# RWKV front on one Trainium2 core: the sigmoids of gates and decays in three rounds of two banks, up to four steps earlier, apart from lane 0's exponentials

## What is computed

```python
for d in range(2):                       # two directions
    w_log = -softplus(-(w0[d] + tanh(xw @ w1[d]) @ w2[d])) - 0.5
    decay = exp(-exp(w_log))             # = exp(-exp(-0.5) * sigmoid(...))
    a = sigmoid(a0[d] + (xa @ a1[d]) @ a2[d])
    k_d = k * (1.0 + (a - 1.0) * k_a)
kk = heads(k * k_k); kk = kk * rsqrt(max(sum(kk * kk), 1e-24))
# scan over 256 context and 512 own tokens, in each direction:
#   sa = S @ -kk_t
#   S = S * decay_t + outer(sa, kk_t * a_t) + outer(v_t, k_t)
#   y = S @ r_t
```

## Time and profile before

| what | value |
|---|---|
| time, median of 3 runs | 3779.27 us (3776.16 to 3779.83) |
| the profiled execution | 3782.2 us |
| its span | 3780.9 us |
| PE, DVE, ACT, POOL busy | 93%, 44%, 29%, 37% |
| granted TensorE clock, mean | 0.974 of full |
| the eight rounds of the RWKV scan | from about 2600 to 3292 us |
| a round, from one product L3413 to the next (2882.27, 2968.43, 3053.64) | 86.2 and 85.2 us |

### The profile page before, as it was taken

One profiled execution on the slowest core, in us unless ns is written; L12 is line 12 of the kernel. 1 busy time (PEld: TensorE's weight loads), 2 busy tenths in 40 slices (PEclk: granted clock), 3 DMA queues, 4 the chain that ended last, 5 costly groups with the idle time before them and its releaser, 6 DMA issues.

```text
span 3780.9 us, 72300 instructions
## 1 busy us (share of the span) xinstructions
PE 3527.5 (93%) x31740; PEld 2276.1 (60%) x31740; DVE 1656.9 (44%) x2942; ACT 1101.6 (29%) x2087; POOL 1389.0 (37%) x1239
## 2 busy tenths in 40 slices
PE   7998899999999989898999998999889888889998
PEld 3755674344554555554555554456667677658887
DVE  1246561465531234444242426524566665333334
ACT  3153331322205633423000002114555455220002
POOL 1230640233312245665324333344344444144443
PEclk9999899999999999999999999999999999999999
DMA  5341005311112135311111111331000000122222
GB/s 191 131 141 34 2 14 190 128 48 48 45 56 73 34 125 178 122 34 45 56 56 62 61 50 50 106 113 51 16 17 17 17 17 4 61 67 88 90 90 67
DMA packets 196434, 263.77 MB, mean 70 GB/s; under 512 B 6135, under 2 KB 151671, under 8 KB 194072
## 3 DMA queue, kind: packets, MB, share of 16 engines
q1 hardware_dynamic: 188960, 241.74, 19.2%
q10 hardware_dynamic: 7160, 17.41, 1.2%
HBM read 246.55 MB, written 12.58 MB: 69 GB/s over the span
## 4 chain that ended last, share of the span: by engine, by line
PE 55%; ACT 6%; DVE 4%; issue 2%; POOL 1%; DMA 0%; ACTq 0%; DVEq 0%; POOLq 0%
PE ps L241 44%; PE ps L3274 2%; PE ps L794 2%; ACT mem L871 1%; PE ps L385 1%; PE ps L821 1%; PE ps L809 1%; PE ps L492 1%; DVE mem L852 1%; ACT mem L3209 1%; PE ps L3833 1%; PE ps L3816 1%; ACT mem L881 0%; PE ps L501 0%; PE ps L3824 0%
## 5 line engine op out<-in xcount | busy, mean ns | idle before, releaser
L241 PE MATMUL ps<-mem 64*64 64x64 f32 (+4 forms) x25120 | 2620.6, 296 | 101.0 <-ACT mem L3209 28.3
L241 PEld LDWEIGHTS ps<-mem 64*64 64x64 f32 (+1 forms) x25120 | 1704.1, 151 | 1024.6 <-issue 522.9
L3139 POOL TENSOR_TENSOR mem<-mem 128x256 f32<-128x256 f32 (+1 forms) x264 | 230.6, 887 | 323.0 <-ACT mem L3709 167.3
L889 POOL TENSOR_SCALAR mem<-mem 128x768 f32<-128x768 f32 (+2 forms) x128 | 219.0, 1724 | 199.8 <-DVE mem L855 199.7
L2384 POOL TENSOR_TENSOR mem<-mem 128x512 f32<-128x512 f32 (+1 forms) x80 | 100.7, 1259 | 443.2 <-PE ps L241 367.2
L2397 ACT ACTIVATE mem<-ps 128x384 f32<-128x384 f32 (+1 forms) x80 | 35.6, 446 | 777.9 <-PE ps L241 735.6
L599 POOL TENSOR_TENSOR mem<-mem 128x512 f32<-128x512 f32 (+1 forms) x72 | 75.2, 1060 | 419.5 <-ACT mem L594 416.4
L2408 DVE TENSOR_TENSOR mem<-mem,ps 128x384 f32<-128x384 f32 (+1 forms) x80 | 39.9, 499 | 414.5 <-PE ps L241 414.5
L3274 PE MATMUL ps<-mem 128*128 128x128 f32 x960 | 168.3, 292 | 14.7 <-DVE mem L3198 11.0
L3198 DVE TENSOR_TENSOR mem<-mem,ps 128x256 f32<-128x256 f32 (+1 forms) x220 | 110.4, 514 | 127.7 <-PE ps L241 126.9
L3207 ACT ACTIVATE mem<-ps 128x256 f32<-128x256 f32 (+1 forms) x220 | 101.3, 460 | 188.0 <-PE ps L3274 187.7
(11 more groups left out here) (322 smaller groups left out, 3976.8 us busy)
## 6 DMA issues: line engine op xcount, KB each, us to landing
mem<-i_mod_w SPq DMA_DIRECT2D x48, 1024.0 KB, 6.9
mem<-i_ffn_wg SPq DMA_DIRECT2D x22, 1024.0 KB, 5.3
mem<-i_ffn_wu SPq DMA_DIRECT2D x22, 1024.0 KB, 5.4
mem<-i_e_w_in SPq DMA_DIRECT2D x16, 1024.0 KB, 6.1
mem<-i_o_w_in SPq DMA_DIRECT2D x16, 1024.0 KB, 5.4
mem<-i_ffn_wd SPq DMA_DIRECT2D x16, 1024.0 KB, 5.0
mem<-i_e_mod_w SPq DMA_DIRECT2D x12, 1024.0 KB, 12.3
mem<-i_o_mod_w SPq DMA_DIRECT2D x12, 1024.0 KB, 7.2
```

The source lines that it names most:

```text
L241: ins = e.h.matmul(out, l, r, start=(i == 0), stop=(i == n - 1))
L889: K.pool.h.tensor_scalar(w, w, stat(i, o, 1), None, MUL).then_inc(*nm.up(tag, i, o))
L3139: K.pool.h.tensor_tensor(m3(self.slot(l)), self.lraw, bm(C(K, f"cm{self.d}", l, 64), 2 * self.np), MUL).then_inc(*self.mk.up(key, l))
```

## The change

For hp 1 to 7 the six sigmoid rounds of a front stand otherwise, in three rounds that use both banks each:

- step 24: both lanes' gates of the own tokens, in banks 6 and 7 (two steps earlier);
- step 26: lane 0's decays, 128x512 in bank 6 and 128x256 in the first half of bank 7, and lane 0's gate of the context in columns 256 to 511 of bank 7 (decays three steps earlier, gate two);
- step 28: the same for lane 1 (decays three steps earlier, gate in its old step), and behind it on ACT the table load (three steps earlier).

Step 31 keeps lane 0's exponentials alone. On DVE lane 0's sums go from step 30 to 28, `kd0` and `kd1` from 31 to 29; `rt` and all behind it, and POOL's whole list, keep their steps. As a bank-7 tile is now written by two matmuls, the second decay sigmoid waits for the later of them (the gate). The front of hp 0 has the same order as before.

The diff, cut where code is only moved into a helper:

```diff
@@ front_pe
+        if hp:
+            for _ in range(3):
+                yield
+            yield from self.sigmoids_pe(hp)
+            return
         for _ in range(5):
             yield
...
-            for _ in range(2 if hp and d == 0 else 6):
+            for _ in range(6):
                 yield
+    def gate_pe(self, hp, d, ri, bk, at):
+        ds, (r0, rn) = slice(64 * d, 64 * d + 64), RNG[ri]
+        self.K.pe.h.matmul(self.K.ps[bk][:, at:at + rn], self.part(hp)[1][ds, :], self.ha[ds, r0:r0 + rn], start=True, stop=True).then_inc(*self.fp.up(hp, d, "a", ri))
...
+    def sigmoids_pe(self, hp):
+
+        K, fa = self.K, self.fa
+        for d in range(2):
+            vacant(K, 6 + d)
+            self.gate_pe(hp, d, 0, 6 + d, 0)
+            K.busy[6 + d] = [(fa, (hp, d, "a", 0))]
+        for d in range(2):
+            yield
+            yield
+            vacant(K, 6)
+            self.decay_pe(hp, d, 0, 6)
+            K.busy[6] = [(fa, (hp, d, "w", 0))]
+            vacant(K, 7)
+            self.decay_pe(hp, d, 1, 7)
+            self.gate_pe(hp, d, 1, 7, 256)
+            K.busy[7] = [(fa, (hp, d, "w", 1)), (fa, (hp, d, "a", 1))]
@@ front_act
-        for _ in range(4):
-            yield
-        for ri, (r0, rn) in enumerate(RNG):
+        for _ in range(2 if hp else 4):
+            yield
+        for d in range(2):
+            self.gate_act(hp, d, 0, self.banks(hp, "a")[d], 0)
+        yield
+        yield
+        if hp:
             for d in range(2):
...
-        self.decay_act(hp, 0)
-        yield
-        yield
-        if hp:
-            self.decay_act(hp, 1)
+                self.decay_act(hp, d, 6, 7)
+                self.gate_act(hp, d, 1, 7, 256)
+                if d:
+                    log_and_exp(K)
+                yield
+                yield
+            yield
...
         for d in range(2):
             e3, c = m3(ep), 63 * (1 - d)
-            if not (hp and d):
+            if not hp:
                 log_and_exp(K)
@@ decay_act
-            A.wait_ge(*fp.at(hp, d, "w", ri))
+            A.wait_ge(*(fp.at(hp, d, "a", 1) if hp and ri else fp.at(hp, d, "w", ri)))
@@ front_dve
-        for _ in range(5):
+        for _ in range(3 if hp else 5):
             yield
...
             V.h.scalar_tensor_tensor(out=L["kd"], in0=L["kd"], scalar=1.0, in1=k, op0=ADD, op1=MUL).then_inc(*fd.up(hp, d, "kd1"))
             yield
+            if hp and d == 0:
+                yield
+                yield
             V.wait_ge(*fa.at(hp, d, "ep"))
```

More of the change, by code:

```diff
@@ L3422, in front_pe @@
             for d in range(2):
[L3423 to L3427, removed]
+                vacant(K, self.first["a"][2 * ri + d])
+                self.gate_pe(hp, d, ri, self.first["a"][2 * ri + d], 0)
+                K.busy[self.first["a"][2 * ri + d]] = [(fa, (hp, d, "a", ri))]
             yield
@@ L3431, in front_pe, with decay_pe @@
         for d in range(2):
-            ds = slice(64 * d, 64 * d + 64)
-            for ri, (r0, rn) in enumerate(RNG):
[L3434 to L3437, removed]
-            for _ in range(2 if hp and d == 0 else 6):
-                yield
+            for ri in range(2):
+                vacant(K, self.first[f"w{d}"][ri])
+                self.decay_pe(hp, d, ri, self.first[f"w{d}"][ri])
+                K.busy[self.first[f"w{d}"][ri]] = [(fa, (hp, d, "w", ri))]
+            for _ in range(6):
+                yield
+    def gate_pe(self, hp, d, ri, bk, at):
+        ds, (r0, rn) = slice(64 * d, 64 * d + 64), RNG[ri]
+        self.K.pe.h.matmul(self.K.ps[bk][:, at:at + rn], self.part(hp)[1][ds, :], self.ha[ds, r0:r0 + rn], start=True, stop=True).then_inc(*self.fp.up(hp, d, "a", ri))
+    def decay_pe(self, hp, d, ri, bk):
+        ds, (r0, rn) = slice(64 * d, 64 * d + 64), RNG[ri]
+        self.K.pe.h.matmul(self.K.ps[bk][:, 0:rn], self.part(hp)[0][ds, :], self.hw[ds, r0:r0 + rn], start=True, stop=True).then_inc(*self.fp.up(hp, d, "w", ri))
+    def sigmoids_pe(self, hp):
[14 more added lines that the diff above has]
+            K.busy[7] = [(fa, (hp, d, "w", 1)), (fa, (hp, d, "a", 1))]
     def values_pe(self, hp):
@@ L3491, in front_act @@
         if hp:
-            self.decay_act(hp, 1)
+            for d in range(2):
+                self.decay_act(hp, d, 6, 7)
[5 more added lines that the diff above has]
+            yield
+        else:
+            for d in range(2):
+                self.gate_act(hp, d, 1, self.first["a"][2 + d], 0)
+            yield
+            self.decay_act(hp, 0, *self.first["w0"])
+            yield
+            yield
         for d in range(2):
             e3, c = m3(ep), 63 * (1 - d)
-            if not (hp and d):
+            if not hp:
                 log_and_exp(K)
```

17 lines of the change are left out of this document (8 added, 9 removed).

## The result

The changed kernel took 3756.48 us, the median of 4 runs (3755.29 to 3761.26), against 3779.55 for the kernel before, the median of 4 (3776.16 to 3782.21). The profiled execution took 3761.3 us, the slowest of the four. Here and in the experiments, four single executions of 4125 to 12505 us, in the slow state, are left out of every median and ratio.

The account below looks back on a forecast made before the run. TensorE, 93% busy, was taken as the bound, with its waits, chiefly for ScalarE's copies, to be cut. Saving 1.84 us a round, 12.9 over seven, taken as 12, less 1, gave 3779.3 - 11 = 3768; range 3762 to 3776.5.

Parts of the forecast that it names:

- Gates at step 24: Moving the gates between rb and the turn bt saves TensorE's 0.16 us wait a round; cost 0, room 1.1 us.
- The slower rival (ScalarE stuck): ScalarE, waiting at step 24 for the turns, reaches the gates late and holds TensorE: 14 us slower, 3793; chance 0.07.
- Lane 0 at step 26: Lane 0's decays and gate before level 1, with VectorE's sums of 1.81 us behind them: cost 0, room 2.3 us.
- the port rival: VectorE's moved sums and GpSimd's masks lock each other out; level 1's subtraction 1.3 us late, 9 of 12 us lost, 3776; chance 0.10.
- Lane 1 at step 28: New TensorE wait of 0.4 us before level 2's turn; ScalarE just in time for level 2's first copy, no room.
- Exponentials at step 31: Exponentials alone before level 3's copy, taken as 0.1 us over; waits of 2.15 and 0.29 become 0.26 + 0.1.
- Level 5: TensorE's wait of 0.49 us for level 4's subtraction, before level 5's turn, was kept; it could vanish.
- Instructions: TensorE's "issue" gaps, where it waits for instructions, might take back some saved time: 1 us charged over seven rounds.
- More: Rival: nothing new waits at level 4, so 16 us are gained, 3763; chance 0.13.
- the fetch: Rival: TensorE's waits for instructions grow by what the levels save, leaving 0 to 3 us of gain, 3777; chance 0.12.
- the two deductions: The saving of 12.9 us was taken as 12 for small waits already hidden, then lessened by about 1 us for instruction supply.

Follow-up runs that it names:

- e3: The changed kernel with VectorE's steps put back as before (lane 0's sums at step 30, kd0 and kd1 at 31): 3779.90 us, 1.0015 to the kernel before.
- e2: The changed kernel with the table load put back at step 31, ahead of lane 0's exponentials: 3765.39 us, 0.9956 to the kernel before.
- e7: The changed kernel with lane 0's q0 one step earlier, in the step of rt: 3756.73 us, 0.9958 to the kernel before.
- e4: The kernel before with lane 0's exponentials moved from step 31 to 33, and VectorE's rt, q0, kd one step later: 3772.15 us, 0.9969 to the kernel before.
- e0: The kernel before, unchanged, timed and profiled once more: 3779.92 us, 1.0001 to the kernel before.
- e10: The changed kernel with three more loads of different tables in one place, ahead of lane 0's exponentials at step 31: 3789.80 us, 1.0032 to the kernel before.
- e11: The changed kernel with seven more loads of alternating tables, spread in four pieces before the copies of levels 2 to 5: 3782.95 us, 1.0014 to the kernel before.

## Why the prediction was wrong in size

The mechanism and the place were right; the sum left out a term. By its own steps:

- **Gates at step 24: right.** The 0.16 us for the copy of k is gone, and ScalarE's wait for the turns bt is 1.09 us with nobody behind it. The slower rival (ScalarE stuck) did not come about.
- **Lane 0 at step 26: right in cost, wrong in duration.** The sums took 3.16 us and not 1.81; the room of 2.3 us held them. My argument against the port rival, that GpSimd is done with masks 2 by then, did not hold: four masks run beside the sums. What the rival said of the sums is true, and its price is not, because it put their end later than they end. That the rival's mechanism was near shows e3: with VectorE's work two steps later it takes back the whole gain.
- **Lane 1 at step 28: right.** A new wait of 0.35 us at level 2 (forecast 0.40). "No room" was right as well: the load ends at 2818.04, the copy starts at 2818.05. e2 says what the load costs at its old step.
- **Exponentials at step 31:** forecast 0.1 over, measured nothing over. The copy starts 0.70 us after the turn.
- **Level 5:** forecast 0.49, measured 0.27; e7 took the rest. GpSimd's chain moved forward by some 0.2 us more against the levels than I had reckoned: when `q0` starts, `b` has 0.22 us to go instead of 0.43, and `q0` takes 1.02 instead of 1.25.
- **Instructions: right in that nothing was given back.** I charged 1 us and "issue" did not rise.
- **The step that failed** is "In rounds 1, 4, 6 and 7 one of the small waits is smaller or hidden already, so I take 12". The observation was true and its reading false. The waits there are hidden because TensorE runs at half rate behind the stall, and that makes these rounds longer, not shorter: 86.2 to 86.5 us against 84.4 and 84.9. It should have been a term of its own with the other sign; the sum had nothing in its place. No rival had it either: the only one on that side, *More*, stopped at 16 us. The profile showed it, in products of 32 at 1.13 us where all others take 0.69; I read the waits between rows and not the durations in them.

The sum as it should have stood: waits 7 x 2.2 = 15.4 (forecast 12.9, taken as 12); the clock, in 4 to 7 rounds 1 to 1.9 us each, taken as 1.3, 5 to 9; nothing for the fetch; together 20 to 25, with 23 measured. Of the 12 us that the forecast lacked, 2.5 are waits that were put too small (level 5 most of all), 2 the two deductions, and the other 7 or 8 are left for the clock. Its term is an estimate: the 1.0 and 1.2 come from the same rounds of the kernel before in two profiles, the 1.9 from its rounds 6 and 7 against the change. It has two independent witnesses at equal idle time: e4 against e0, 8.5 us in six intervals, and e10 against e11, 7.2.

The Trainium skill ("TensorE: Matmul & The Clock Gate", HAM oscillation — how this bites in real kernels) says that waits which come back in each step of a loop can bring the clock down anew each time, so that it is paid once a step. The rows agree: 11 of 14 rounds behind 2.15 us, and all 14 behind 2.37 and 3.32. The waits in the page's example are longer than 2.15 us, so by the page alone one would have thought this stall too short; the measurement decides. Weighed together with the durations behind the stall, the rule would have added a term of 5 to 9 us to my 11 and put the forecast between 3759 and 3763.

Not settled is which rounds of the kernel before are hit (four in one execution, seven in another). That the first of the six intervals is some 2 us longer than the next in both kernels lies in "issue": 4.3 us against 2.3 in the kernel before, 4.7 against 2.4 in the changed one.

## What to carry to other kernels

On an engine whose clock can fall, a stall is priced by its length and by its effect on what runs behind it: before a sum is made over waits, compare the durations of equal instructions right behind the long waits with those elsewhere. Here the same 31 us of idle time cost about 7 us more in seven long pieces than in many short ones. And when work is moved to an earlier step on one engine, the engine that consumes it has to move with it: left at its old step, VectorE lost all that the other two had gained.

## What was not expected of the hardware

- In the levels the clock behind idle time went by the length of one piece and not by the sum: 31.7 us with seven pieces of 3.3 gave a stretch at 1.2 GHz in all seven rounds, 31.0 us in pieces up to 0.8 gave none. Behind a single stall of 2.15 us it came in 11 rounds of 14.
- Such a stretch costs less than half its length. In the kernel before TensorE is 1.2 to 1.4 us longer busy in a round with one of 3.4 us, and some 0.6 us of waits go.
- Table loads of the same table, written directly behind one another, come out as one instruction of 1.28 us; loads of different tables stay apart, 1.28 us each.
- A VectorE multiplication of 128x512 with both inputs in SBUF takes 0.77, 1.23 or 2.30 us as GpSimd's instruction has 0.22, 0.68 or 1.76 us to go when it starts; the scan of the sums goes from 1.81 to 3.16 us for two beside the masks.
